# A decoder block on eight cores: modulation loads on another queue, a half own block, and a new place for the halo tile

## The reference

```
mod = silu(c) @ ada_w + ada_b            -> shift1, scale1, gate1, shift2, scale2, gate2
h   = rms_norm(x) * (1 + scale1) + shift1
q, k, v, p, g_attn, g_pool = split(h @ w_in)      # 8 heads of 64; p 512; gates 1024 each
q, k = per-head rms_norm(q), rms_norm(k)
attn: blocks of 256 keys; each query sees its own block (causal) and the 3 past
      blocks with the highest q . mean(k); T5 relative bias by distance; softmax
pool: trailing means over 2/4/8/16 tokens minus the token, a 128x128 matrix per group
merged = sigmoid(g_attn) * (attn @ w_a) + sigmoid(g_pool) * (pool @ w_p)
x   = x + gate1 * (merged @ w_out)
h2  = rms_norm(x) * (1 + scale2) + shift2
u   = causal depthwise conv3(h2 @ w_up)            # 2 x 2816 wide
x   = x + gate2 * ((silu(u_g) * u_v) @ w_down)
```

## Time and profile before

| | us |
|---|---|
| median of 3 runs | 1965.44 (1964.96 to 1969.68) |
| the profiled execution | 1962.53 |
| its span on the core shown | 1961.0 |
| the eight cores' spans | 1943.7 to 1961.0 |
| PE busy | 1742.9, 89% |
| ACT, DVE, POOL busy | 1075.4, 1092.0, 657.1 |

### The profile page before, as it was taken

One profiled execution on the slowest core, in us unless ns is written; L12 is line 12 of the kernel. 1 busy time (PEld: TensorE's weight loads), 2 busy tenths in 40 slices (PEclk: granted clock), 3 DMA queues, 4 the chain that ended last, 5 costly groups with the idle time before them and its releaser, 6 DMA issues.

```text
span 1961.0 us, 39762 instructions; the slowest of 8 cores (1943.7 to 1961.0 us)
## 1 busy us (share of the span) xinstructions
PE 1742.9 (89%) x13621; PEld 1187.6 (61%) x13700; DVE 1092.0 (56%) x1486; ACT 1075.4 (55%) x1395; POOL 657.1 (34%) x609
## 2 busy tenths in 40 slices
PE   7768999989987989796989999989976999999998
PEld 3335555555554767665666777754435888887443
DVE  1556555555555564645364554426765888887222
ACT  1436454544535978776777988953234666665000
POOL 1778667667671000000000000005764444442000
PEclk9889999999997999998989999989997999999999
DMA  9894444434455141424232130414759534340332
GB/s 257 161 184 138 115 120 130 116 110 123 119 115 123 46 89 29 114 58 109 64 79 51 18 58 2 86 44 138 198 129 167 51 36 41 37 41 11 107 115 95
DMA packets 245742, 187.49 MB, mean 96 GB/s; under 512 B 158293, under 2 KB 211925, under 8 KB 244457
## 3 DMA queue, kind: packets, MB, share of 16 engines
q1 hardware_dynamic: 186378, 154.93, 28.6%
q0 software_dynamic: 59168, 30.02, 12.8%
HBM read 170.77 MB, written 44.12 MB: 110 GB/s over the span
## 4 chain that ended last, share of the span: by engine, by line
PE 75%; issue 5%; DMA 5%; ACT 4%; POOL 4%; DVE 4%; SPq 1%; DVEq 0%; ACTq 0%; POOLq 0%
PE psum L387 72%; ACT arena L395 3%; PE psum L391 3%; POOL arena L403 2%; DMA arena<-ada_w 2%; POOL arena L441 2%; SPq L400 1%; DVE arena L403 1%; DMA arena<-w_in 1%; DVE psum L403 1%; ACT arena L419 1%; DMA arena<-SGS 1%; DMA arena<-xw 1%; DVE arena L414 1%; POOL arena L439 1%
## 5 line engine op out<-in xcount | busy, mean ns | idle before, releaser
L387 PE MATMUL psum<-arena 128*128 128x256 bf16 (+7 forms) x12493 | 1661.4, 291 | 158.9 <-ACT arena L395 73.2
L387 PEld LDWEIGHTS psum<-arena 128*128 128x128 bf16 (+3 forms) x12572 | 1119.9, 99 | 685.4 <-issue 265.8
L395 ACT ACTIVATE arena<-psum 128x1024 bf16<-128x1024 f32 (+2 forms) x731 | 636.9, 962 | 355.5 <-PE psum L387 282.9
L403 POOL TENSOR_TENSOR arena<-arena 128x1024 bf16<-128x1024 f32 (+2 forms) x211 | 347.4, 1653 | 315.8 <-ACT arena L395 144.9
L414 DVE SCALAR_TENSOR_TENSOR arena<-psum,arena 128x512 f32<-128x512 f32 (+1 forms) x354 | 266.1, 753 | 85.2 <-PE psum L387 65.1
L403 DVE TENSOR_TENSOR arena<-psum,arena 128x512 f32<-128x512 f32 (+5 forms) x245 | 151.2, 636 | 278.6 <-PE psum L387 146.0
L414 DVE SCALAR_TENSOR_TENSOR arena<-arena 128x1024 f32<-128x1024 f32 (+3 forms) x137 | 209.2, 1532 | 73.6 <-DMA arena<-ada_w 32.7
L395 ACT ACTIVATE arena<-psum,arena 128x512 f32<-128x512 f32 (+4 forms) x220 | 162.2, 737 | 140.8 <-PE psum L387 138.8
L400 POOL DMA_DIRECT2D arena<-wba x1 | 0.8, 768 | 615.6 <-PE psum L387 615.6
L395 ACT ACTIVATE arena<-arena 128x512 bf16<-128x512 f32 (+3 forms) x174 | 144.3, 829 | 88.7 <-DVE arena L403 52.3
L441 POOL TENSOR_TENSOR arena<-arena 128x8 f32<-128x8 f32 (+1 forms) x148 | 185.5, 1257 | 15.8 <-POOL arena L439 0.6
(11 more groups left out here) (24 smaller groups left out, 146.2 us busy)
## 6 DMA issues: line engine op xcount, KB each, us to landing
arena<-xw SPq DMA_DIRECT2D x80, 512.0 KB, 4.3
arena<-ada_w SPq DMA_DIRECT2D x32, 512.0 KB, 4.8
arena<-wup POOLq DMA_DIRECT2D x44, 256.0 KB, 5.3
arena<-ada_w SPq DMA_DIRECT2D x8, 1024.0 KB, 11.4
arena<-w_in POOLq DMA_DIRECT2D x8, 1024.0 KB, 17.7
VS<-arena SPq DMA_DIRECT2D x32, 256.0 KB, 4.2
KS<-arena SPq DMA_DIRECT2D x32, 256.0 KB, 4.2
SGS<-arena SPq DMA_DIRECT2D x8, 1024.0 KB, 6.1
```

The source lines that it names most:

```text
L387: P.op('tensor', lambda e: e.matmul(out, lhsT=lhsT, rhs=rhs, start=start, stop=stop), R, W, dur=d, mode=(rk(lhsT.shape[0]), rk(fs(lhsT)), ...
L395: P.op('scalar', lambda e: e.activation(out=out, in_=in_, func=func, **kw), R, W, dur=edur('scalar', fs(in_)) + (0.1 if 'accum_out' in kw ...
L403: P.op(eng, lambda e: e.tensor_tensor(out=out, in0=in0, in1=in1, op=op), R, W, dur=edur(eng, fs(out)))
```

## The change

Five edits.

- The loads of `ada_steps` go to GpSimd's queue instead of sync's.
- The eight loads of K and V for the next head stand one by one at groups 5, 11, ... 47 instead of all at group 4.
- The second 128 keys of the own block meet only the second 128 queries: the product, the mask, the exponential (896 columns instead of 1024 in a group that ends in an own unit) and the product with V are shorter. The bias tables shrink from 640 to 512 columns; the memory after them is laid out so that `attnT` stays behind 161.5 KB.
- The halo (`hq` and tile 16 of `out_a`) comes ahead of the last chunk of the output projection instead of within and behind it. The up projection begins with sp 0 to 2 of the first three feature pairs, then takes sp 3 of each.
- `w_own` waits for the last operation of the `stageB` one tile earlier; the first one for `G1rep`.

```diff
         STT(G1rep, psum[:, 1024:2048], 1.0, g1r, ALU.add, ALU.mult, [('ps', 2), ('ps', 3), 'g1r'], ['G1rep'])
+        g1k[0] = P.last
...
             if pos % 2 == 0 and pos < 12:
-                w_own(pos // 2, P.last)
+                w_own(pos // 2, g1k[0])
+            g1k[0] = P.last
...
                 for ktl in range(2):
                     kt_ = 2 * n + ktl
-                    MM(bank(bk, 256, off=ktl * 256), Kaug[hbuf][0:96, kt_ * 128:(kt_ + 1) * 128],
-                       Qaug[hbuf][0:96, s * 256:(s + 1) * 256], True, True, Kk, [('ps', bk)])
+                    q0 = 128 if kind == 'own' and ktl else 0
+                    MM(bank(bk, 256 - q0, off=ktl * 256), Kaug[hbuf][0:96, kt_ * 128:(kt_ + 1) * 128],
+                       Qaug[hbuf][0:96, s * 256 + q0:(s + 1) * 256], True, True, Kk, [('ps', bk)])
                 if kind == 'own':
-                    TT('vector', bank(bk), bank(bk), Tnear[h % 3][:, 0:512], ALU.add, [('ps', bk), NK[h % 3]], [('ps', bk)])
+                    TT('vector', bank(bk, 384), bank(bk, 384), Tnear[h % 3][:, 0:384], ALU.add, [('ps', bk), NK[h % 3]], [('ps', bk)])
...
-            nu = len(units)
-            ACT(PT[pi].rearrange("p k q -> p (k q)")[:, 0:nu * 512], psum[:, sp * 1024: sp * 1024 + nu * 512], AF.Exp,
-                [('ps', 2 * sp + i) for i in range(nu)], [('PT', pi)])
+            nc_ = 512 * len(units) - (128 if units[-1][2] == 'own' else 0)
+            ACT(PT[pi].rearrange("p k q -> p (k q)")[:, 0:nc_], psum[:, sp * 1024: sp * 1024 + nc_], AF.Exp,
+                [('ps', 2 * sp + i) for i in range(2)], [('PT', pi)])
...
                 for ktl in range(2):
-                    MM(o, Vaug[hbuf][:, 2 * n + ktl, :], PT[pi][:, 2 * i + ktl, :], first and ktl == 0, last and ktl == 1,
+                    q0 = 128 if kind == 'own' and ktl else 0
+                    MM(o[:, q0:], Vaug[hbuf][:, 2 * n + ktl, :], PT[pi][:, 2 * i + ktl, 0:256 - q0], first and ktl == 0, last and ktl == 1,
...
-                    DMA('sync', ada2[kt % 2], adaw_v[kt, :, pc * 1024:(pc + 1) * 1024], (), [('ada2', kt % 2)], 'ada2%d' % (kt % 2))
+                    DMA('gpsimd', ada2[kt % 2], adaw_v[kt, :, pc * 1024:(pc + 1) * 1024], (), [('ada2', kt % 2)], 'ada2%d' % (kt % 2))
...
-                    for j in range(4):
-                        p2_k(h + 1, j)
-                        p2_v(h + 1, j)
+                if gi % 6 == 5 and 5 <= gi < 53 and h + 1 < 8:
+                    j_ = gi // 6
+                    (p2_k if j_ % 2 == 0 else p2_v)(h + 1, j_ // 2)
...
             pq = pool_parts(ci + 2) if ci + 2 < 4 else []
+            if ci == 3:
+                while hq:
+                    hq.pop(0)()
+                outb.pop(0)()
+                outb.append(out_a(16))
             for tl in range(4):
                 outb.append(out_a(4 * ci + tl))
...
-                elif hq:
-                    for _ in range(3):
-                        if hq:
-                            hq.pop(0)()
                 if len(outb) >= 2:
                     outb.pop(0)()
-        outb.append(out_a(16))
...
         for fp in range(22):
-            for sp in range(4):
+            if fp == 0:
+                for f_ in range(3):
+                    for sp in range(3):
+                        up(f_, sp)
+            for sp in range(3 if fp < 3 else 0, 4):
                 up(fp, sp)
```

More of the change, by code:

```diff
@@ L300, in build_nc @@
     gqcol_d = din("gqcol", [128, 1])
-    traw_d = din("traw", [128, 8, 640])
-    cmask_d = din("cmask", [128, 640])
+    traw_d = din("traw", [128, 8, 512])
+    cmask_d = din("cmask", [128, 512])
     rb31_d = din("rb31", [128, 8])
@@ L556, in build_nc @@
         CP('scalar', shift1rep, psum[:, 0:1024], [('ps', 0), ('ps', 1)], ['shift1'])
+        g1k = [None]
         STT(G1rep, psum[:, 1024:2048], 1.0, g1r, ALU.add, ALU.mult, [('ps', 2), ('ps', 3), 'g1r'], ['G1rep'])
+        g1k[0] = P.last
         def w_own(i, after):
@@ L741, in build_nc @@
         gm = T2b([17], F32, 'gm')
-        cmask = T2b([640], F32, 'cmask')
+        cmask = T2b([512], F32, 'cmask')
         rb31 = T2b([8], F32, 'rb31')
-        Tnear = [T2b([640], F32, 'TnearA'), T2b([640], F32, 'TnearB'), Alloc(126, 129)([640], F32, 'TnearC')]
+        Tnear = [T2b([512], F32, 'TnearA'), T2b([512], F32, 'TnearB'), Alloc(126, 129)([512], F32, 'TnearC')]
         NK = ['TnearA', 'TnearB', 'TnearC']
@@ L748, in build_nc @@
         Ocp = [T2b([256], F32, 'Ocp') for _ in range(2)]
-        attnT = T2b([4, QT], BF16, 'attnT')
-        Qaug1 = T2b([QP], BF16, 'QaugB', parts=96)
+        T2d = Alloc(161.5, 182.5)
+        attnT = T2d([4, QT], BF16, 'attnT')
+        Qaug1 = T2d([QP], BF16, 'QaugB', parts=96)
         Kaug = [Kaug0, Kaug1]
@@ L970, in p2_group @@
                     kt_ = 2 * n + ktl
[L971 to L972 removed]
+                    q0 = 128 if kind == 'own' and ktl else 0
+                    MM(bank(bk, 256 - q0, off=ktl * 256), Kaug[hbuf][0:96, kt_ * 128:(kt_ + 1) * 128],
+                       Qaug[hbuf][0:96, s * 256 + q0:(s + 1) * 256], True, True, Kk, [('ps', bk)])
                 if kind == 'own':
[L974 removed]
+                    TT('vector', bank(bk, 384), bank(bk, 384), Tnear[h % 3][:, 0:384], ALU.add, [('ps', bk), NK[h % 3]], [('ps', bk)])
                 elif kind == 'adj':
[L976 removed]
+                    TT('vector', bank(bk, 128, off=256), bank(bk, 128, off=256), Tnear[h % 3][:, 384:512], ALU.add,
                        [('ps', bk), NK[h % 3]], [('ps', bk)])
[L978 to L980 removed]
+            nc_ = 512 * len(units) - (128 if units[-1][2] == 'own' else 0)
+            ACT(PT[pi].rearrange("p k q -> p (k q)")[:, 0:nc_], psum[:, sp * 1024: sp * 1024 + nc_], AF.Exp,
+                [('ps', 2 * sp + i) for i in range(2)], [('PT', pi)])
             return pi
@@ L1003, in p2_halo @@
                    [KA(hbuf, kt_ // 16), KA(hbuf, 'oh'), QA(hbuf, 'q1'), QA(hbuf, 'm2')], [sk[kt_ // 32]])
-            tn = Tnear[h % 3][:, 0:512].rearrange("p (k q) -> p k q", q=256)[:, :, 254:256]
+            tn = Tnear[h % 3][:, 128:384].rearrange("p (k q) -> p k q", q=128)[:, :, 126:128]
             for sl in range(8):
@@ L1042, in tail_ld @@
                 acc(7)
-                DMA('sync', ada2[0][0:1], adab_d[:, pc * 1024:(pc + 1) * 1024], (), [('ada2', 0)], 'ada20')
+                DMA('gpsimd', ada2[0][0:1], adab_d[:, pc * 1024:(pc + 1) * 1024], (), [('ada2', 0)], 'ada20')
                 if pc == 4:
-                    DMA('sync', ada2[1], g2rep_d, (), [('ada2', 1)], 'ada21')
+                    DMA('gpsimd', ada2[1], g2rep_d, (), [('ada2', 1)], 'ada21')
             def finish():
@@ L1413 @@
     qq = np.arange(256)[None, :]
-    dd = np.concatenate([qq - kl, qq - 128 - kl, qq[:, 0:128] + 128 - kl], axis=1)
+    dd = np.concatenate([qq - kl, qq[:, 0:128] - kl, qq[:, 0:128] + 128 - kl], axis=1)
     bidx = _t5_bucket_np(dd)
-    traw = np.zeros((128, 8, 640), np.float32)
+    traw = np.zeros((128, 8, 512), np.float32)
     for h in range(8):
```

## The result

The changed kernel takes 1982.6 us against 1965.2: 1.009 of the time before, 95% interval 1.0064 to 1.0115, slower by 0.9%.

What follows compares the result with a forecast made beforehand. TensorE, at work for 89% of the span, was taken as the bound, with gaps in attention and before the up projection. Terms 32 + 0 + 7 + 17 + 2 = 58 us off 1962.5, plus 2.9 for the median, gave 1907; range 1885 to 1942.

Steps and rivals of the forecast that it cites:

- Modulation weights, 32: Attention: modulation loads on GpSimd's queue no longer wait to be issued and arrive in time; saves 32 us, bounds 11 and 44.
- the 80 to 86 us: Attention: expected length in the new profile of the stretches of the four heads that load modulation weights.
- Rivals C: Attention: modulation loads on GpSimd's queue are as late as now, delayed by V packets; 1939 us, chance 0.14.
- D: Attention: modulation loads land as late as the input weights, 17.7 us; 34 us slower, 1999 us, chance 0.06.
- K and V, 0: Attention: K and V loads in eight parts leave the planner's dependences the same; cost and gain 0.
- Own block, 7: Attention: 64 own units lose 128 columns in products, mask addition and exponential; saves 7 us, bounds 3 and 15.
- rival E: The planner's new order hurts elsewhere, for instance GpSimd's in the first stage; up to 30 us lost, 1937, chance 0.02.
- Halo ahead, 17: Before the up projection: idle time falls from 25.3 to about 9 us; saves 17 us, bounds 6 and 22.
- What can cover it: Before the up projection: banks 1 to 5 are free, so 32 to 40 up products run early, 3.6 to 4.4 us.
- no gap later: Up projection: after one gap of under 10 us before it, the new profile would show no further gap.
- rival B: Seam gives little: gate loads stall VectorE and TensorE, or fourth weight pair is 10 us late; 1922 us, chance 0.12.
- Input weights, 2: First stage, 60 to 150 us: earlier input weight loads fill time before but collide with tiles; gain 2, bounds -8 and +8.

Runs made afterwards that it cites:

- e_ada: Kernel before with only the attention's modulation loads moved from sync's to GpSimd's queue: ratio 0.9835, -32 us.
- e_best1: Kernel before with modulation loads on GpSimd's queue and the shorter own half planned with the old durations: ratio 0.9751, -49 us.
- e_newplan: Kernel before, every instruction at its old size, but planned with the shorter own half's durations: ratio 1.0168, +33 us.
- e_adaown: Kernel before with modulation loads on GpSimd's queue and the shorter own half at its new planned order: ratio 1.0006, +1 us.
- e_seam: Kernel before with only the halo tile ahead of the last chunk and the up projection's first calls reordered: ratio 1.0057, +11 us.
- e_g1k: Kernel before with only the own-tile input weight loads waiting for one tile earlier: ratio 0.999.
- e_onecost: Kernel before, no instruction changed; 64 own-block score products planned at 0.07 us in place of 0.12: ratio 1.0039, +8 us.
- s_warm: e_seam with 32 unread products of 512 columns added behind the halo's steps: ratio 1.0025, +5 us against the kernel before.

## Why the prediction was wrong, by its steps

**Modulation weights, 32.** Right in size and mechanism, by e_ada: the wait for issue is gone, no long mask wait is left, and the loads (37, not 36) land in 4.8 us, not 7 to 8. The four heads came out near the 80 to 86 us only where the order was kept (e_ada by the medians: 83.9 to 86.7; e_best1: 81.2 to 86.9); in the changed kernel they take 88.7 to 95.2. Rivals C and D fall. With 4.8 us beside fp32 accumulations, nothing was seen here of the delay that the Trainium skill, "SBUF — State Buffer", "SBUF: two separate sides", warns of; no row shows whether these accumulations run in the two-port mode that it speaks of.

**K and V, 0.** Right, by the identical program.

**Own block, 7.** This is the step that failed. It costed shorter instructions in the old order. But their durations are also the planner's input, and the order that came out costs 33 us by itself (e_newplan). The prediction used the planner's readiness rule for K and V and for the up products and did not apply it here; rival E named a new order, but at a chance of 0.02, for GpSimd's in the first stage. The size was too small too: with the order kept the part gives 22 (interval 15 to 28), over the upper bound of 15; the attention alone is 17.5 us shorter in the profiled execution. In the two last heads it is 3.0 us a head (78.1 to 75.1, 74.4 to 71.4). A worked-out reading, not tested by itself: if product, mask addition, exponential and product of the own unit stand in series, 50 + (697 - 565) + (1040 - 917) + 50 = 355 ns, times 64 is 22.7 us. The prediction charged only one engine's saving where by this reading the savings add.

**Halo ahead, 17.** Failed in two places. "What can cover it" held: 48 up products ran early. But the claim that 9 us of idle time are left of 25.3 was made of the end alone, where the rows show a gap of 15.6; that the other 10 us would vanish had no row behind it. The halo's own chain was costed with at most two gate waits at its new place, and it took the gap along, where the clock then fell on full-size work. And "no gap later" was wrong: behind the early products TensorE waited 2.73 and 1.03 us for VectorE's convolution steps. What rival B said (it gives little) was nearer, though not by its mechanism, and the fourth weight pair was not late: in the whole up projection TensorE waits for nothing but these 3.8 us.

**Input weights, 2.** Nothing that can be told from 0, inside its bounds.

**The range.** Its lower end does not come out of its own terms: 1907 less 12 and 5 is 1890, not 1885. That changes nothing here, since the time lies above its upper end.

Put together with the measured terms: e_adaown +1, e_seam +11, e_g1k -2 make +10; the whole measured +18 (interval 13 to 23). The half-widths of the first two are 6 and 5 us, so the 8 us between can't be told from chance. By the table the changed kernel is e_adaown in the attention and 9 us longer behind it.

## What to carry to other kernels

Where a planner orders the instructions by modelled durations, every edit that changes a duration is two edits: time the new shapes at the old order and the old shapes at the new order before judging either. Here a change worth -22 us was measured as +29 because of an order that nobody had chosen. Before a short tile is moved ahead of full-size ones to hide its chain, count the stalls at the place where it goes, and what the clock does to the work behind them.

## What was not expected of the hardware

The half clock can cost as much as the stalls themselves: in e_newplan's attention 16.4 us more idle time came with 20.5 us more of clock loss. But the sum of the idle time does not set it. The changed kernel's attention has 10.1 us less idle time than before and 12.0 us more clock loss, e_onecost's 3.3 less and 6.9 more; so it matters how the gaps are spread, and by what rule was not measured. In the seam, 7 us of products that nobody reads went with a gain of 6 us (e_seam 1.0057, s_warm 1.0025), with the granted clock at 0.83 in place of 0.60 over 30 us.
